# One core, two transformer blocks: a modulation matrix in three transfers, host-packed gate columns, another order of projections, and one modulation sum moved to VectorE

## The reference, cut to what matters

```
ada = silu(c) @ w_ada + b_ada                  # w_ada: 1024 x 6144, c: one row of 1024
shift_a, scale_a, gate_a, shift_m, scale_m, gate_m = split(ada, 6)     # parts 0 to 5
h = rmsnorm(x, g_mix) * (1 + scale_a) + shift_a
gq, gk, gv, gr, gg, mq, mk, mv = split(h @ w_in)       # gg: 16 columns, the gate rank
# gated linear attention from gq, gk, gv, gg (4 heads), softmax attention from mq, mk, mv (8 heads)
x = x + gate_a * (concat(gla_out * silu(gr), attn_out) @ w_out)
h = rmsnorm(x, g_mlp) * (1 + scale_m) + shift_m
```

## Time and profile before

| what | value |
|---|---|
| median of three runs | 1814.32 us |
| the profiled execution, span from first to last instruction | 1812.1 us |
| median less that span | 2.2 us |
| TensorE matmul busy | 1250.0 us (69%) |
| VectorE busy | 295.1 us (16%) |
| ScalarE busy | 229.5 us (13%) |
| GpSimd busy | 50.1 us (3%) |
| HBM read | 647.36 MB, 358 GB/s over the span |
| chain that ended last | DMA 61%, TensorE 32%, VectorE 4%, the rest 3% |

### The profile page before, as it was taken

The page is one execution under the profiler, slowest core; times in us unless marked ns, Lnnn a source line. Parts: engine busy times, 40 slices in busy tenths (PEclk is TensorE's granted clock), DMA queues, the critical chain, the costliest instruction groups (busy, mean ns, idle before and its releaser), DMA issues.

```text
span 1812.1 us, 23305 instructions
## 1 busy us (share of the span) xinstructions
PE 1250.0 (69%) x10190; PEld 723.6 (40%) x10190; DVE 295.1 (16%) x586; ACT 229.5 (13%) x533; POOL 50.1 (3%) x101
## 2 busy tenths in 40 slices
PE   6999999999997655646555564654565555556555
PEld 4577888888573322213122221222222222212222
DVE  1325300018832100101000000100000010100001
ACT  1332221021143101001010100101010110101010
POOL 0001000002010000000000000000000000000000
PEclk9999999999998777877777787777778777877878
DMA  9774643423258999999999999999999999999998
GB/s 362 264 263 194 240 166 151 182 98 144 112 224 364 429 425 432 430 433 434 433 434 423 437 430 432 435 437 431 423 437 430 431 433 439 431 425 436 428 432 347
DMA packets 48576, 649.18 MB, mean 358 GB/s; under 512 B 3992, under 2 KB 6536, under 8 KB 31256
## 3 DMA queue, kind: packets, MB, share of 16 engines
q1 hardware_dynamic: 45296, 643.90, 84.3%
q10 hardware_dynamic: 3032, 3.72, 0.7%
q0 software_dynamic: 208, 1.00, 0.1%
HBM read 647.36 MB, written 1.25 MB: 358 GB/s over the span
## 4 chain that ended last, share of the span: by engine, by line
DMA 61%; PE 32%; DVE 4%; issue 1%; ACT 1%; SPq 1%; POOL 0%; DVEq 0%; PEldq 0%; ACTq 0%; POOLq 0%
DMA ring<-in_w 60%; PE ps L1257 32%; DVE arena L1057 3%; DMA ring<-in_w_ada 1%; SPq L361 1%; PE ps L1484 0%; ACT arena L713 0%; ACT hT L543 0%; POOL arena L469 0%; DVE arena L1059 0%; DVE arena L1026 0%; DVE arena L1206 0%; DVE arena L1172 0%; DVE arena L1098 0%; DVE arena L1046 0%
## 5 line engine op out<-in xcount | busy, mean ns | idle before, releaser
L1257 PE MATMUL ps<-ring,table 128*32 128x352 f32 x4032 | 439.9, 607 | 344.0 <-DMA ring<-in_w 342.0
L1257 PEld LDWEIGHTS ps<-ring,table 128*32 128x32 f32 x4032 | 156.1, 141 | 623.4 <-issue 344.6
L1257 PE MATMUL ps<-ring,arena 128*32 128x256 f32 (+1 forms) x2818 | 197.8, 439 | 147.8 <-DMA ring<-in_w 147.5
L1257 PEld LDWEIGHTS ps<-ring,arena 128*32 128x32 f32 (+1 forms) x2818 | 103.6, 126 | 244.2 <-issue 149.0
L1257 PE MATMUL ps<-hT,ring 128*128 128x256 f32 (+1 forms) x880 | 190.8, 381 | 3.1 <-PE ps L1257 1.6
L1257 PE MATMUL ps<-arena,ring 128*128 128x256 f32 (+1 forms) x800 | 174.5, 380 | 1.9 <-ACT arena L656 1.1
L1257 PEld LDWEIGHTS ps<-hT,ring 128*128 128x128 f32 (+1 forms) x880 | 163.8, 189 | 28.8 <-issue 6.1
L1257 PEld LDWEIGHTS ps<-arena,ring 128*128 128x128 f32 x800 | 151.7, 190 | 23.2 <-issue 3.3
L1257 PE MATMUL ps<-arena 32*128 32x256 f32 (+11 forms) x544 | 91.1, 379 | 28.2 <-DVE xT L1249 12.2
L778 ACT ACTIVATE arena<-ps 128x256 f32<-128x256 f32 x16 | 6.1, 383 | 734.7 <-PEq L1867 734.7
L1249 DVE TENSOR_TENSOR xT<-xT,ps 128x512 f32<-128x512 f32 x64 | 41.9, 685 | 342.5 <-PE ps L1257 342.4
(11 more groups left out here) (233 smaller groups left out, 561.0 us busy)
## 6 DMA issues: line engine op xcount, KB each, us to landing
ring<-in_w SPq DMA_DIRECT2D x76, 5632.0 KB, 32.9
ring<-in_w SPq DMA_DIRECT2D x19, 2816.0 KB, 28.4
ring<-in_w SPq DMA_DIRECT2D x35, 1408.0 KB, 31.2
ring<-in_w_ff SPq DMA_DIRECT2D x8, 4096.0 KB, 14.0
ring<-in_w_ada SPq DMA_DIRECT2D x6, 4096.0 KB, 16.9
ring<-in_w_in SPq DMA_DIRECT2D x3, 4096.0 KB, 14.0
ring<-in_w_in SPq DMA_DIRECT2D x5, 2048.0 KB, 19.6
ring<-in_w_out SPq DMA_DIRECT2D x2, 4096.0 KB, 13.4
```

Of the source, the lines that this page charges most:

```text
L1257: return pe.matmul(o, w, x, start=first, stop=last)
```

## The change: what it does

- Unit ada1 comes in three transfers (chunks 0 to 2, 3 to 5, 6 and 7), each with its own semaphore; `ada_part(1)` waits for each before its first chunk. All other units come as before.
- The 16 gate-rank columns of `w_in` are laid out by the host as a 128 x 256 array padded with zeros and come as 1 KB rows in one contiguous transfer, instead of 64-byte rows into a buffer that GpSimd had filled with zeros. SP no longer waits for that filling. TensorE waits for this transfer after gq0 instead of before it.
- TensorE's order becomes gq0, gg, gq1, rel, gk0, `ada_part(0)`, gk1; `ada_turn(0)` is done inside gk1, after half of its matmuls.
- Part 3 is summed on VectorE: `ada_sums(3)` stands right behind `ada_sums(2)` and ahead of `ada_rows(2)`; `ada_added(3)` stands on TensorE behind mk3; `ada_rows(3)` moves ahead of the heads. The place of `ada_part(3)` behind the first scores goes to gr1, that of gr1 to gr2, and the filler of pair 1 keeps `ada_turn(3)` and gr3.
- The list of `bank_plan` follows that order, and the counts of some semaphores change.

```diff
-FILLER = {0: ("gr1",), 1: ("at3", "gr2", "gr3"), 2: ("ada4",), 3: ("at4",)}
+FILLER = {0: ("gr2",), 1: ("at3", "gr3"), 2: ("ada4",), 3: ("at4",)}
...
-    order = ["n_in", "ada1", "at1", "gg", "gq0", "gq1", "rel", "ada0", "gk0", "at0", "gk1", "bias", "gv0", "bt", "gv1", "z"]
+    order = ["n_in", "ada1", "at1", "gg", "gq0", "gq1", "rel", "gk0", "ada0", "gk1", "at0", "bias", "gv0", "bt", "gv1", "z"]
...
-        part2, part5 = ar(2048, 1024), ar(8192, 1024)
+        part2, part3, part5 = ar(2048, 1024), ar(3072, 1024), ar(8192, 1024)
...
-                sp.dma_start(unit[:, :, 0:n], src).then_inc(unit_in[i % 3], 16)
+                if name == "ada1":
+                    for q in range(2):
+                        sp.dma_start(unit[:, 3 * q:3 * q + 3, :], src[:, 3 * q:3 * q + 3, :]).then_inc(s[f"ada1_in{q}"], 16)
+                    sp.dma_start(unit[:, 6:8, :], src[:, 6:8, :]).then_inc(unit_in[i % 3], 16)
+                else:
+                    sp.dma_start(unit[:, :, 0:n], src).then_inc(unit_in[i % 3], 16)
                 if name == "win_a":
-                    sp.wait_ge(s["zero_set"], 3)
-                    sp.dma_start(ring[:, WG:WG + C * 32].rearrange("p (c n) -> p c n", c=C)[:, :, 0:RANK],
-                                 rows(T["w_in"], 1536, RANK)).then_inc(unit_in2, 16)
+                    sp.dma_start(ring[:, WG:WG + C * 32], T["gate_rank"]).then_inc(unit_in2, 16)
...
-            nc.gpsimd.memset(ring[:, WG:WG + C * 32], 0.0).then_inc(s["zero_set"], 1)
...
             ada_sums(2, part2)
+            ada_sums(3, part3)
             ada_rows(2)
             ada_cols(2)
...
             dve.sem_inc(s["S_set"], 1)
+            ada_rows(3)
...
                 divided(2 * p + 1)
-                if p == 0:
-                    ada_rows(3)
...
-                for c in range(c0, c1):
+                for c in range(C):
+                    if k == 1 and c == 6:
+                        wait_unit(pe, "ada1")
+                    elif k == 1 and c % 3 == 0:
+                        pe.wait_ge(s[f"ada1_in{c // 3}"], 16)
...
-            pe.wait_ge(unit_in2, 16)
...
             proj("gq0", w, 0, hT, s["t0_set"])
+            pe.wait_ge(unit_in2, 16)
...
+            proj("gk0", w, 2 * P, hT)
             ada_part(0)
-            proj("gk0", w, 2 * P, hT)
-            ada_turn(0)
-            proj("gk1", w, 3 * P, hT)
+            proj("gk1", w, 3 * P, hT, at=lambda c: ada_turn(0) if c == 4 else None)
...
+            ada_added(3, part3, 3)
             wait_unit(pe, "win_r")
...
             scores(0)
-            fill("ada3")
+            fill("gr1")
```

More of the change, by code:

```diff
@@ L67, in bank_plan @@
 def bank_plan():
-    order = ["n_in", "ada1", "at1", "gg", "gq0", "gq1", "rel", "ada0", "gk0", "at0", "gk1", "bias", "gv0", "bt", "gv1", "z"]
+    order = ["n_in", "ada1", "at1", "gg", "gq0", "gq1", "rel", "gk0", "ada0", "gk1", "at0", "bias", "gv0", "bt", "gv1", "z"]
     held = {label: set(order[order.index(label) + 1:order.index("bt") + 1]) for label in ("gg", "gq0", "gq1", "gk0", "gk1")}
     held["gv0"] = {"bt"}
-    order += ["mv0", "mv1"] + [f"mq{i}" for i in range(4)] + ["mk0", "ada2", "mk1", "mk2", "at2", "mk3"]
+    order += ["mv0", "mv1"] + [f"mq{i}" for i in range(4)] + ["mk0", "ada2", "mk1", "mk2", "at2", "mk3", "ada3"]
     order += ["klT", "att0", "att1", "kv0", "kv1", "gr0", "o0", "o1", "gs0", "gs1"]
-    order += ["sc0", "sc1", "ada3"]
+    order += ["sc0", "sc1", "gr1"]
     for p in range(MH // 2):
@@ L276, in build @@
         s = {name: sem(name) for name in """
-            x_in table_in ident_in rest_in mv_in shift_set gbias_set grs_set xg_set pv_set unit_used w_used const_set e_set attz_set attd_set
+            x_in table_in ident_in rest_in mv_in ada1_in0 ada1_in1 shift_set gbias_set grs_set xg_set pv_set unit_used w_used const_set e_set attz_set attd_set
             att_set hid_used consts2_in conv_set cm_set acc_set gg2_set u2_set den_set epsd_set r1_set xr_set rsq_set qc_set cmean_set crec_set
@@ L286, in build @@
             mixm_set h2_set rs16i_set qn_set rt_set qf_set mixa_set aff_set rank_set
-            sc_used hTe_set zero_set""".split()}
+            sc_used hTe_set""".split()}
         def bk(label):
@@ L414, in _ @@
             nc.gpsimd.memset(eps, EPS).then_inc(s["const_set"], 1)
-            nc.gpsimd.memset(ring[:, WG:WG + C * 32], 0.0).then_inc(s["zero_set"], 1)
-            nc.gpsimd.memset(wgate, 0.0).then_inc(s["zero_set"], 1)
-            nc.gpsimd.memset(gbias[:, 4:5], 0.0).then_inc(s["zero_set"], 1)
+            nc.gpsimd.memset(wgate, 0.0).then_inc(s["const_set"], 1)
+            nc.gpsimd.memset(gbias[:, 4:5], 0.0).then_inc(s["const_set"], 1)
             nc.gpsimd.memset(scanm, 1.0).then_inc(s["const_set"], 1)
-            pool.wait_ge(s["const_set"], 3)
+            pool.wait_ge(s["const_set"], 5)
             nc.gpsimd.memset(scanm.rearrange("p (n t) -> p n t", t=CH)[:, :, 0:1], 0.0).then_inc(s["const_set"], 1)
@@ L508, in _ @@
             act.dma_start(ident[:, :], T["table1"][:, 0:P]).then_inc(s["ident_in"], 16)
-            act.wait_ge(s["zero_set"], 3)
+            act.wait_ge(s["const_set"], 4)
             for dst, src in (*((wgate[32 * j:32 * j + RANK, :], T["w_gla_gate"]) for j in range(4)), (relst, T["rel_bias"]),
@@ L853, in _ @@
             link(V.scalar_tensor_tensor(zz, zz, 0.0, tt, ALU.min, ALU.subtract))
-            dve.wait_ge(s["const_set"], 4)
+            dve.wait_ge(s["const_set"], 6)
             link(V.tensor_tensor_scan(bb, scanm, zz, 0.0, ALU.mult, ALU.add))
@@ L867, in _ @@
             V.tensor_tensor(kl, kl, gk, ALU.mult).then_inc(s["gla_set"], 1)
-            dve.wait_ge(s["const_set"], 5)
+            dve.wait_ge(s["const_set"], 7)
             V.scalar_tensor_tensor(qb1[CH:P, :], qb[CH:P, :], GDK ** -0.5, gq[CH:P, :], ALU.mult, ALU.mult)\
@@ L1276, in _, with ada_part @@
             norm_sum("n_in", sq0, s["sq0_set"])
-            def ada_part(k, c0=0, c1=C):
-                if c0 == 0:
+            def ada_part(k):
+                if k != 1:
                     wait_unit(pe, f"ada{k}")
-                    wait_emptied(pe, f"ada{k}")
+                wait_emptied(pe, f"ada{k}")
                 w = unit_ap(f"ada{k}", C, D)
-                for c in range(c0, c1):
+                for c in range(C):
[3 more added lines that the diff above has]
+                        pe.wait_ge(s[f"ada1_in{c // 3}"], 16)
                     for j in range(4):
@@ L1287, in ada_part @@
                                  w[:, c, j * DG:(j + 1) * DG], c == 0, c == C - 1)
-                if c1 == C:
-                    finish(f"ada{k}", ins)
+                finish(f"ada{k}", ins)
             def ada_added(k, part, n):
@@ L1565, in _ @@
                 if u == 0:
-                    ada_added(5, part5, 3)
+                    ada_added(5, part5, 4)
             for u in range(4):
@@ L1902, in laid_out @@
     x_turned = np.ascontiguousarray(given["x"].reshape(S, C, P).transpose(2, 1, 0))
-    return {"table0": table0, "x_turned": x_turned}
+    rank = np.zeros((P, C, 32), np.float32)
+    rank[:, :, 0:RANK] = given["w_in"][0, :, 1536:1536 + RANK].reshape(C, P, RANK).transpose(1, 0, 2)
+    return {"table0": table0, "x_turned": x_turned, "gate_rank": rank.reshape(P, C * 32)}
 def tables():
```

1 line of the change is left out of this document (removed).

## The result

The changed kernel takes 1823.98 us (median of 4 runs, 1821.28 to 1825.12), against 1814.28 us for the kernel before on the same chip. The ratio is 1.0049 with a 95% interval of 1.0037 to 1.0061: slower by 8.9 us (6.7 to 11.1) by the ratio; the two medians are 9.7 us apart. The forecast was 1820.3 us, its range 1812.3 to 1824.5. The profiled execution took 1825.12 us with a span of 1823.3 us, 1.1 us above the median of the runs.

A forecast was written before the change was run, and what follows sets the result against it. Transfers bound the start to 34.88 us, engines releasing each other to 585.44, then expert-weight streaming; earlier steps carry through one for one. -0.5 - 1.86 + 0.82 + 5.2 + 2.6 - 0.25 = +6.0 us, giving 1820.3 us, range 1812.3 to 1824.5.

The forecast's parts named there:

- the forecast's 0.46: Whole kernel: chance given to the forecast itself, +6.0 us, 1820.3 us, with its own range of 1818 to 1822.3.
- Rival (a): Pair 1 of the heads: TensorE's second idle time lowers the clock too; +8.5 us in all, 1822.8; chance 0.22.
- ada1 in three transfers: Start, `ada_part(1)`: the 0.65 us wait for ada1 goes, win_a is late next; gain taken as 0.5 us.
- Gate columns: Start: SP is freed early, but the DMA engines are full to 44 us; 0, at most a few tenths.
- gk0 ahead of ada0: Start, TensorE: gk0 runs until after ada0's landing, so the wait of 1.86 us goes whole.
- `ada_added(3)`: TensorE ahead of klT: added matmuls cost 0.64 us and a gap of 0.18, +0.82 on the path.
- The wait: `ada_turn(2)` ahead of mk3: TensorE waits 5.2 us, as VectorE waits for ada3 and sums part 3 first.
- The clock: mk3, behind the idle time at `ada_turn(2)`: TensorE runs at half clock, losing 2.6 us (bounds 0 and 3.62).
- The heads: Pair 1 without gr2: VectorE bounds it, 0.25 us gained; 3.4 us of TensorE idle time without a clock fall.
- the forecast's start: Start of the kernel: gains of 0.5 and 1.86 us, so gk1 to mk2 come 2.36 us earlier.

The follow-up runs named there:

- e3: Changed kernel with two lines exchanged: VectorE does `ada_rows(2)` ahead of `ada_sums(3)`; 1816.15 us, ratio 1.0006 to the kernel before.
- e6: Kernel before with only gk0 put ahead of ada0 and `ada_turn(0)` inside gk1; 1812.79 us, ratio 0.9990 to the kernel before.
- e1: Kernel before with only part 3's sums moved to VectorE, its column added and fillers as in the change; 1821.9 us, ratio 1.0048.
- e2: Changed kernel with part 3 put back on TensorE and fillers as before, so only the start's changes stay; 1812.34 us, ratio 0.9988 to the kernel before.
- e4: Changed kernel in which ScalarE waits for ada3 before issuing the eight `rel_rows` transfers; 1817.08 us, ratio 1.0014 to the kernel before.
- e5: Changed kernel with ten useless TensorE products before the wait of `ada_turn(2)`; 1820.53 us, ratio 1.0031 to the kernel before.
- e11: e3 with 6 useless TensorE products in pair 1, where it stood idle; 1814.66 us, ratio 0.9995 to the kernel before.
- e8: e3 with gr2 put back into pair 1 and no filler in pair 0; 1811.75 us, ratio 0.9989 to the kernel before.
- e9: e3 with 14 useless TensorE products in pair 1, where it stood idle; 1816.75 us, ratio 1.0014 to the kernel before.

## Why the prediction came out

The measured time lies in the range of 1812.3 to 1824.5 us, but not in the 1818 to 1822.3 that went with the forecast's 0.46, and the +6.0 us lie below the measured interval. Rival (a), at +8.5 us and 0.22, came nearer. The mechanism of the loss was foreseen; that the time stayed in the range with one step wrong is owed to the width of the range. By its own steps:

- **ada1 in three transfers, -0.5.** Right: the wait is gone and win_a is next, landing at 23.66 us (23.3 was forecast); gq0 starts 0.22 us earlier in the change's profile, 0.48 in e3's. In the medians a step of this size can't be seen.
- **Gate columns, 0.** Right in its cost, wrong in its reason: SP was said to be freed early, but its issue of the contiguous columns still took 10.93 us. Nothing waited for it.
- **gk0 ahead of ada0, -1.86.** Right: e6 alone gives -1.8 us, and no wait is left before ada0. With the term before it, mk1 starts 2.09 us earlier in e3's profile (94.27 against 96.36), where 2.36 was forecast. In the changed kernel's profile it doesn't show, since there the clock fell in gq0 and took 1.72 us back. That this can happen the prediction didn't consider; e1's profile shows that it happens without the start's change, and e2 that the start is a gain in the median all the same.
- **`ada_added(3)`, +0.82.** Measured +0.96.
- **The wait, +5.2.** Measured +4.59, by the mechanism named: ada3 took 19.6 us where 20.1 was taken, and e3 and e4 each take the wait away. In the profile the sums of part 2 began at 79.00 us, 0.2 us earlier than before, so the clock of before was still the right one to reckon in.
- **The clock, +2.6.** Measured +2.92; e5 shows it to be a cost of its own.
- **The heads, -0.25.** This step failed: measured +1.22. What it said of VectorE was right, the transposes behind the idle time come 0.4 us sooner. But I took the end without a fall of the clock for the 3.4 us of idle time, and it fell, in the changed kernel and in e1, e3, e4 and e5 alike, each time behind 3.38 us. (The fall behind the 2.25 us of the earlier trace rows stands in the stretch after the row shown there: 0.56 from 637.50 to 638.00 us.) Rival (a) had the mechanism, at 2.5 us; its price was about 1.5 (1.22 and the 0.25 not gained), as the part of ada4 lost 1.05 us and the rows before it half a microsecond. e11 shows the mechanism.

The Trainium skill's page "TensorE: Matmul & The Clock Gate" (section "Part 1: The HAM clock gate") was cited ahead for rival (a), as it lets the clock of an idle engine drop. The rows of pair 1 agree with it, with 4.71 us against 3.66.

With the forecast's start and the measured sizes of the other terms the sum is -2.36 + 0.96 + 4.59 + 2.92 + 1.22 = +7.3 us, against 8.9 (6.7 to 11.1) measured. The rest, 1.6 us, is within the interval. In the profile it is more than covered by the start's 48 slow matmuls and the 1.70 us near 480 us, but in how many executions either is there no run here shows. Whether slow matmuls at the start are likelier in the changed kernel, where TensorE waits 2.37 us before gq0 and not 1.20, stays open: with about the same wait e3 (2.10 us) and e8 (1.95) kept the full clock, while e1 lost it at 1.20.

## What to carry over

When work moves to another engine, read what stands behind it in that engine's written order: here a sum that nobody needed yet was put ahead of a copy that TensorE needed next, and exchanging two lines was worth 7.8 us. Price a wait on TensorE twice, once as the wait and once as the work behind it at the lower clock, and a stretch that loses its filler likewise. Compare the moved work with leaving it: here the start alone was as good as the mended whole. When a transfer is late, see who shares the DMA engines with it: the transfers in the way were the ones that could wait.

## What was unexpected of the hardware

- SP's issue of the gate columns took 12.31 us before and 10.93 us after, though the transfer went from many short rows to one contiguous row for each of 128 partitions. In both kernels it stands behind 6 MB that were just issued (4 MB of ada1, 2 of win_a), so the shape of the transfer was not the main thing that held SP; what did is not shown. The row of the kernel before:

```profile
1.95 12.31 SPq L361 DMA_DIRECT2D ring<-in_w_in  x1
```

- The idle time right ahead of gq0 doesn't tell whether the clock falls there. It fell to 0.50 behind 1.20 us (e1), 1.48 (e9), 1.57 (e2) and 2.37 (the change, 10.06 us for 48 matmuls), and stayed at 1.00 behind 1.20 (before, e6) and 1.75 to 2.10 (e11, e5, e4, e8, and e3 with 8.37 us). Behind 3.38 us in pair 1 it fell in all five profiles that have it, but at different prices: from klT to y0 it takes 44.61 us in e11, where the clock was kept up, 45.88 to 46.03 in e3, e4, e1 and the change, and 47.13 in e5. The Trainium skill's page "TensorE: Matmul & The Clock Gate" (section "Part 1: The HAM clock gate") says of the slow matmuls at a kernel's start that their number differs between runs of one kernel. The 10.06 and 8.37 us, of two kernels that are alike up to there, agree with that.
- The eight `rel_rows` transfers of 128 KB are dear: by themselves, from 89 to 94 us in e4, they keep the DMA engines full (share 1.04) at 148 GB/s, and beside them ada3 takes 7.0 us longer.
- Useless products cost nothing that could be measured where they fit the idle time, and kept the clock at 1.00: mk3 at 3.62 us in e5 instead of 6.31.
